# GpSimd adds up the squares for three more norms, and TensorE makes one product for each

## The reference

```python
def rms_norm(x, g):
    y = x * lax.rsqrt(jnp.mean(x * x, axis=-1, keepdims=True) + EPS)
    return y * g
def adaln(x, g, shift, scale):
    return rms_norm(x, g) * (1.0 + scale) + shift
def gated_residual(x, y, g, gate):
    return x + gate * rms_norm(y, g)
for layer in range(DEPTH):
    h = adaln(x, g[0], sh, sc)
    y = mixer(h)                                 # state-space in layer 0, attention in layer 1
    x = gated_residual(x, y, g[1], gt)
    x = gated_residual(x, conv_ffn(adaln(x, g[2], shf, scf)), g[3], gtf)
```

## Time and profile before

| what | value |
|---|---|
| median of three executions | 2809.28 us |
| profiled execution, first to last instruction (span) | 2802.0 us |
| what lies around the span (2809.28 less 2802.0) | 7.3 us |
| TensorE matmul busy | 2577.8 us, 92% of the span |
| VectorE busy | 1502.1 us, 54% |
| ScalarE busy | 794.2 us, 28% |
| GpSimd busy | 270.0 us, 10% |
| mean granted TensorE clock | 0.951 of 2.4 GHz |

### The profile page before, as it was taken

How to read it: one execution, slowest core, us unless ns; L and a number is a source line. 1 busy time by engine, 2 the same in 40 slices (tenths; PEclk the granted TensorE clock), 3 DMA queues, 4 the chain that set the end, 5 groups by cost and what they waited for, 6 DMA issues and landing times.

```text
span 2802.0 us, 39635 instructions
## 1 busy us (share of the span) xinstructions
PE 2577.8 (92%) x16849; PEld 2357.3 (84%) x16849; DVE 1502.1 (54%) x2284; ACT 794.2 (28%) x1385; POOL 270.0 (10%) x269
## 2 busy tenths in 40 slices
PE   7889999998999898996999999789999969999996
PEld 7885967987898787995999999678666859999995
DVE  1447364247523767236662564489566566624644
ACT  1333332210121024213232232232444333322221
POOL 0004022013201320111000000200000120000002
PEclk7899999999999999997999999899899979999998
DMA  5220411320132012331222222111000102222221
GB/s 215 94 92 11 139 46 66 120 83 9 50 118 81 9 68 91 120 137 37 76 71 81 68 76 80 54 46 61 5 1 1 46 19 72 76 83 69 76 76 45
DMA packets 51214, 193.87 MB, mean 69 GB/s; under 512 B 5824, under 2 KB 5824, under 8 KB 50400
## 3 DMA queue, kind: packets, MB, share of 16 engines
q1 hardware_dynamic: 47664, 175.48, 18.7%
q0 software_dynamic: 2224, 13.24, 1.3%
q10 hardware_dynamic: 1152, 2.62, 0.2%
HBM read 183.72 MB, written 7.60 MB: 68 GB/s over the span
## 4 chain that ended last, share of the span: by engine, by line
PE 82%; DVE 13%; ACT 3%; issue 1%; DMA 0%; POOL 0%; SPq 0%; DVEq 0%; ACTq 0%
PE pg L448 56%; PE pg L425 6%; PE pg L734 3%; PE ps L759 3%; PE ps L600 3%; PE ps L475 2%; DVE rb L1151 2%; PE ps L747 2%; DVE att L1323 1%; DVE xT L1194 1%; DVE hl L1157 1%; DVE wk L1329 1%; PE ps L543 1%; PE ps L547 1%; DVE tp L1327 1%
## 5 line engine op out<-in xcount | busy, mean ns | idle before, releaser
L448 PE MATMUL pg<-hh,whi 128*128 128x320 f32 x2992 | 712.9, 320 | 71.0 <-DVE hl L1157 63.0
L448 PE MATMUL pg<-hl,whi 128*128 128x320 f32 x2992 | 689.3, 312 | 0.0
L448 PE MATMUL pg<-hh,wlo 128*128 128x320 f32 x2992 | 688.4, 312 | 0.0
L448 PEld LDWEIGHTS pg<-hh,whi 128*128 128x128 f32 x2992 | 502.7, 191 | 109.6 <-issue 83.4
L1133 DVE TENSOR_TENSOR wlo<-ring,whi 128x1024 fp32r<-128x1024 f32 x231 | 282.9, 1225 | 475.2 <-ACT whi L802 475.0
L448 PEld LDWEIGHTS pg<-hl,whi 128*128 128x128 f32 x2992 | 507.9, 191 | 0.0
L448 PEld LDWEIGHTS pg<-hh,wlo 128*128 128x128 f32 x2992 | 507.2, 190 | 0.0
L802 ACT CAST whi<-ring 128x1024 fp32r<-128x1024 f32 x231 | 242.3, 1049 | 331.0 <-PE pg L448 224.6
L600 PE MATMUL ps<-wk,kg 128*128 128x128 f32 x1120 | 157.2, 289 | 27.4 <-DVE wk L1329 20.0
L600 PEld LDWEIGHTS ps<-wk,kg 128*128 128x128 f32 x1120 | 137.2, 195 | 47.1 <-DVE wk L1329 40.2
L1151 DVE RECIPROCAL rb<-rt 128x640 f32<-128x640 f32 x29 | 120.4, 4153 | 86.4 <-ACT rt L823 86.4
(11 more groups left out here) (231 smaller groups left out, 3248.0 us busy)
## 6 DMA issues: line engine op xcount, KB each, us to landing
ring<-in_wstream SPq DMA_DIRECT2D x231, 512.0 KB, 3.3
adaring<-in_wada SPq DMA_DIRECT2D x82, 512.0 KB, 3.4
adabig<-in_wada SPq DMA_DIRECT2D x14, 512.0 KB, 15.4
xT<-in_x SPq DMA_DIRECT2D x1, 2560.0 KB, 11.1
yssd_scratch<-ybuf POOLq DMA_DIRECT2D x2, 1280.0 KB, 6.7
xT<-yssd_scratch POOLq DMA_DIRECT2D x1, 2560.0 KB, 10.3
xT<-in_x POOLq DMA_DIRECT2D x1, 2560.0 KB, 11.2
out_y<-xT ACTq DMA_DIRECT2D x8, 320.0 KB, 2.2
```

Of the source, the lines that this page charges most:

```text
L448: last = nc.tensor.matmul(out[:, half], w[:, s % 2, pos, :], a[:, k, half * HALF:(half + 1) * HALF], start=n == 0 and m == 0, stop=n == le ...
```

## The change

Three norms join `POOLED`, and GpSimd's list gains an `add_squares` for each, behind the `normalise` of the residual ahead of it:

```diff
-POOLED = (N_SSD, N_RES0, N_RES1, N_RES2, N_RES3)
+POOLED = (N_SSD, N_RES0, N_FFN0, N_RES1, N_ATT, N_RES2, N_FFN1, N_RES3)
...
-            for a in (N_RES0, N_RES1):
+            for a, b in ((N_RES0, N_FFN0), (N_RES1, N_ATT)):
                 add_squares(a)
                 normalise(a)
+                add_squares(b)
...
             add_squares(N_RES2)
             normalise(N_RES2)
+            add_squares(N_FFN1)
             add_squares(N_RES3)
             normalise(N_RES3)
```

## The result

The changed kernel took 2830.8 us (median of four executions, 2827.7 to 2834.9), against 2809.2 us for the kernel before, measured beside it (2805.2 to 2809.7). The ratio is 1.0082 with a 95% interval of 1.0068 to 1.0097, or 19 to 27 us slower. A second measurement of both gave 1.0089 (1.0075 to 1.0102) with medians of 2831.9 and 2807.4. The forecast was 2839.1, with a range from 2827 to 2846.

What follows compares the result with a forecast made beforehand. VectorE and GpSimd taking turns were taken to set the pace around the norms. Losses of 9.6 + 10.1 + 10.1 = 29.8 us gave a span of 2831.8, plus 7.3 around it 2839.1 us; range 2827 to 2846.

Steps and rivals of the forecast that it cites:

- What bounds the kernel: Around the norms VectorE and GpSimd set the pace; fewer products could return only 1.43 us tail and about 0.8 us wait.
- Turns: In the residual, two-input operations of VectorE and GpSimd wait for each other, about 1.32 us per GpSimd operation.
- The sum of the adds: GpSimd's copy and seven adds per norm, 9.95 us of work sharing turns with VectorE's residual, ending at 1305.7.
- The tail: Behind the last add, TensorE's one product at half clock: 0.14 us to issue, 2.48 to run, 0.02 to the root.
- The three gaps: First normalisation to root at N_FFN0, N_ATT and N_FFN1: 28.8 us each, losing 9.6, 10.1 and 10.1 us.
- rival A: Less contention: adds behave as their median row, or ScalarE and TensorE overlap better; 21.1 us, 2830.4; chance 14%.
- What costs nothing: GpSimd's five DMAs before attention start some 17 us later, with more than 30 us of cover before their reader.
- B: The adds take no turns with VectorE at all; 11.7 us slower, 2821.0; chance 5%.
- C: Not slower: with fewer matmuls in the gaps, TensorE gets full clock for more of the projections; about 2809, chance 2%.
- D: More than the sum: hand-overs of 0.3 us and more low-clock stretches; 37 to 40 us, 2846 to 2849; chance 11%.
- E: The adds are hidden behind something ending later in the gap, so the time stays; chance 2%.
- The signs named ahead: Trace signs: copy right behind the fifth normalisation, additions over 1.5 us beside adds, residual 7 us later, distance near 28.8.

Runs made afterwards that it cites:

- e2: Kernel before, TensorE's eight products kept, with GpSimd making a copy and seven adds of constants behind its normalisations that nothing waits for; ratio 1.0093.
- e7: Kernel before, with GpSimd making one copy and two adds of constants beside VectorE's reciprocal at the three norms; ratio 0.9998.
- e4: Kernel before, with VectorE making all eight normalising products and GpSimd none; 2799.2 us against 2807.4, ratio 0.9973, and 0.9966 when repeated.
- e5: Changed kernel with its adds on GpSimd, but VectorE making all eight normalising products; ratio 1.0069.
- before_again: The kernel before, unchanged, measured and traced a second time; ratio 0.9999, span 2804.2 us.

## Why the prediction was right, and where its sizes were off

*What bounds the kernel.* Right. Taking 84 of 96 matmul records out of the three gaps bought nothing that the adds did not take back several times. One reading was generous: of the 0.8 us put down to the last square's wait for a buffer, shows 0.42 us as ScalarE's wait for TensorE. TensorE's busy time fell by 28 us and the span grew by 31; the page's busy shares point the wrong way here, and the chain of waits names TensorE for time in which it waited for tiles.

*Turns.* Right, and now shown by removing the dependence (e2), by moving a copy and two adds beside the reciprocal, where they cost nothing (e7), and by giving the normalising to VectorE (e4, e5). The turn was sized at 1.32 us, the length of the record of an add alone; e5 shows that it costs VectorE 1.07 to 1.28.

*The sum of the adds.* This is the term that was mis-sized. The prediction put the seventh add's end at 26.2 us behind the first normalisation (1305.7 less 1279.5); it came at 25.4 (1310.3 less 1284.93), 0.8 us less at each norm. The copy (1.17 us with its wait) and the first two adds end within 0.2 us of the forecast, 14.3 behind the start against 14.1. From the third add on, which starts 15.25 us behind the first normalisation against 15.9 forecast, the trace is ahead, by 0.2 to 1.0 us at each further step; the sixth add starts 1.0 us behind the fifth's end, for 1.8 forecast. The likely reason, not tested alone, is that VectorE works undisturbed while GpSimd waits for a square, and that each turn is a little under 1.32.

*The tail.* Right: 0.14 us to issue and 2.47 for four records at the level of 1.2 GHz, the granted clock being 0.50 all through the gap. The stretch of the changed kernel from 1300 to 1310 us (columns as in the earlier trace rows):

```profile
1300.00:1310.00 10.00, 0.00 (x0) 0.00 (x0) 7.40 (x9) 3.06 (x5) 7.53 (x5) 0.50 0.00 0
```

*The three gaps.* Forecast 9.6 + 10.1 + 10.1 = 29.8 us; measured 8.80 + 9.35 + 9.36 = 27.5, inside the 26 to 34 of the forecast.

*From the gaps to the time.* Here the forecast missed by more: the step of the medians was 21.5 and then 24.5 us, for 29.8, and neither lies in its 26 to 34. The stated range from 2827 to 2846 held because it was drawn down over rival A as well, whose 2830.4 is nearest to the time measured; the time alone would have chosen the wrong rival, and only the distances tell them apart. Of the miss 2.3 us lie in the gaps. Some 2 us are what comes back elsewhere; the forecast allowed -1.7 to +3.4 us for the restart of the projection, but no run shows that it is the restart. The remainder is within the scatter of the medians: the base of 2809.28 stood 2 to 4 us above the three later medians of the kernel before, 2807.4, 2806.2 and 2805.7. The 7.3 us that were set around the span are really about 2, since the changed kernel's profiled execution took 2834.9 us for a span of 2832.8 and that of before_again 2806.4 for 2804.2; by that the execution profiled before took an estimated 2804 and was faster than the median. This doesn't touch the step from median to median. In the changed kernel's first trace the low stretch behind N_FFN1 is there again, in its second it is not (granted clock 0.83 and 1.00, columns as in the earlier trace rows):

```profile
2334.00:2344.00 10.00, 8.29 (x44) 7.48 (x43) 8.11 (x15) 5.44 (x9) 0.00 (x0) 0.83 0.18 54
```

```profile
2331.00:2341.00 10.00, 7.83 (x48) 6.81 (x47) 8.49 (x15) 5.85 (x10) 0.00 (x0) 1.00 0.17 54
```

What sets the difference between stretches of the same instructions is open.

*What costs nothing.* The DMAs behind N_ATT started at 1839.4, 25.3 us behind the gap's first product (1814.1) in place of 9.1, so 16 us later for 17 forecast; their reader ran at 1888.3, 48.9 us behind them. Covered, as forecast.

*The rivals.* A and B ask for distances of about 25.9 and 22.7 us to the root, against 28.0: out. C is out by the time; the granted mean, which it wants higher, went from 0.951 to 0.940, though the longer gaps at 0.50 are in that. D is out, since the hand-overs cost less, not more. E is out by the time.

*The signs named ahead.* The copy began at 1294.02, at the end of the fifth normalisation; line 475 had four records of `rt` at half clock; the distance was within 0.8 us of 28.8. The additions of VectorE grew to a mean of 1.30 and 1.02 us, not to over 1.5; the likely reason is that an add is in flight beside only some of them. The residual ended 6.1 us later, for 7 forecast.

## What to carry to other kernels

In a stretch where VectorE works on operations with two operands in SBUF, count each GpSimd operation there at nearly its full length on VectorE's own path (here 1.07 to 1.28 us for an add of 1.31); moving work to GpSimd pays only if it replaces more VectorE time than its turn (here 0.82 us were saved for 1.3), or if it lies beside something that it leaves alone, which here was shown of the reciprocal only. Before matmuls are taken out of a stretch, look whether TensorE is busy there or only waiting with many short records, and add what the first product costs at the low clock that the idle time leaves. Compare stretches of two traces rather than two totals when the effect is about as large as the scatter: the gaps repeated to 0.02 us, while the times of one kernel's executions differed by up to 9.

## What the runs showed of the hardware that I had not expected

VectorE's reciprocal (4.15 us, one operand) and GpSimd's copy and adds ran side by side without touching the reciprocal (e7). The Trainium skill (GPSIMD Engine Reference, section 8) names as the contended case VectorE instructions in a 2-port mode or with two SBUF inputs; e2 and e7 agree, with 10.56 us for six two-input additions that take 2.87 alone, and a reciprocal that kept its 4153 ns: of the 29 in e7, three with company, none took over 4155. The wait of each engine for the other lies inside the recorded duration of its instruction (an add of 1.31 us alone is 1.84 or 2.06 in e5), so that busy time in such a stretch counts the same microseconds on both. And useless products on TensorE made the useful one 1.16 us faster (2.47 to 1.31).
